# Inverse roots of the row norms on ScalarE, and two moves of turned rows, in a four-layer hybrid kernel

## The reference

```python
def rms_norm(x, g):
    xf = x.astype(jnp.float32)
    y = xf * lax.rsqrt(jnp.mean(xf * xf, axis=-1, keepdims=True) + EPS)
    return (y * g.astype(jnp.float32)).astype(x.dtype)
...
def hybrid_layer(x, c_act, positions, norm_w, w_ada, b_ada, w_in, ret_gn_w, w_proj_attn, w_proj_ret, w_out):
...
    h = rmsnorm(x, norm_w) * (1.0 + scale[:, None, :]) + shift[:, None, :]
    proj = h @ w_in
...
    y_ret = o_ret.astype(x.dtype) * jax.nn.silu(zr)
    merged = jax.nn.sigmoid(ga) * (y_att @ w_proj_attn) + jax.nn.sigmoid(gr) * (y_ret @ w_proj_ret)
    return x + gate[:, None, :] * (merged @ w_out)
```

## Time and profile before

| | us |
|---|---|
| median of three executions | 1066.57 |
| profiled execution, device time | 1068.22 |
| profiled execution, span from first to last instruction | 1066.6 |
| TensorE (PE) busy | 1021.5 |
| VectorE (DVE) busy | 691.5 |
| ScalarE (ACT) busy | 565.2 |
| GpSimd (POOL) busy | 346.8 |

### The profile page before, as it was taken

One profiled execution on the slowest core, in us unless ns is written; L12 is line 12 of the kernel. 1 busy time (PEld: TensorE's weight loads), 2 busy tenths in 40 slices (PEclk: granted clock), 3 DMA queues, 4 the chain that ended last, 5 costly groups with the idle time before them and its releaser, 6 DMA issues.

```text
span 1066.6 us, 15450 instructions
## 1 busy us (share of the span) xinstructions
PE 1021.5 (96%) x6084; PEld 901.6 (85%) x6084; DVE 691.5 (65%) x995; ACT 565.2 (53%) x874; POOL 346.8 (33%) x379
## 2 busy tenths in 40 slices
PE   4899999999999899999999989989999999999996
...
GB/s 269 149 157 90 145 104 111 268 212 233 227 129 180 178 265 225 239 197 158 171 213 180 174 173 202 219 137 199 249 213 217 121 138 178 179 157 140 191 143 40
DMA packets 94441, 191.13 MB, mean 179 GB/s; under 512 B 6769, under 2 KB 10097, under 8 KB 94369
## 3 DMA queue, kind: packets, MB, share of 16 engines
...
HBM read 189.07 MB, written 1.05 MB: 178 GB/s over the span
## 4 chain that ended last, share of the span: by engine, by line
PE 88%; ACT 5%; DVE 4%; POOL 1%; issue 1%; POOLq 0%; DVEq 0%; ACTq 0%
PE G L600 15%; PE G L602 15%; PE G L601 14%; PE G L609 8%; PE G L612 8%; PE G L611 8%; PE B L563 2%; PE G L638 2%; PE G L640 1%; PE G L639 1%; ACT AR L1053 1%; ACT WH L1053 1%; DVE WL L1535 1%; PE B L912 1%; PE B L724 1%
## 5 line engine op out<-in xcount | busy, mean ns | idle before, releaser
L1535 DVE TENSOR_TENSOR WL<-RAW,WH 128x1024 fp32r<-128x1024 f32 (+2 forms) x306 | 397.8, 1304 | 257.1 <-ACT WH L1053 256.4
L1053 ACT ACTIVATE WH<-RAW 128x1024 fp32r<-128x1024 f32 (+2 forms) x306 | 319.9, 1050 | 283.7 <-PE G L602 142.9
L600 PE MATMUL G<-WH,HTh 128*128 128x512 f32 (+1 forms) x564 | 227.9, 404 | 3.0 <-DVE WL L1535 2.8
L609 PE MATMUL G<-HTh,WH 128*128 128x256 f32 x768 | 220.1, 287 | 0.3 <-DVE HTl L1595 0.3
L602 PE MATMUL G<-WL,HTh 128*128 128x512 f32 (+1 forms) x564 | 219.1, 388 | 0.0
L601 PE MATMUL G<-WH,HTl 128*128 128x512 f32 (+1 forms) x564 | 218.5, 387 | 0.0
L611 PE MATMUL G<-HTl,WH 128*128 128x256 f32 x768 | 217.7, 283 | 0.0
L612 PE MATMUL G<-HTh,WL 128*128 128x256 f32 x768 | 217.6, 283 | 0.0
L609 PEld LDWEIGHTS G<-HTh,WH 128*128 128x128 f32 x768 | 146.9, 191 | 2.2 <-issue 2.0
L611 PEld LDWEIGHTS G<-HTl,WH 128*128 128x128 f32 x768 | 147.0, 191 | 0.9 <-issue 0.7
L612 PEld LDWEIGHTS G<-HTh,WL 128*128 128x128 f32 x768 | 146.9, 191 | 0.0
...
## 6 DMA issues: line engine op xcount, KB each, us to landing
...
```

The costliest lines, as they stand in the source:

```text
L600: nc.tensor.matmul(o, xh, wh, start=begins, stop=False)
L609: nc.tensor.matmul(o, fh, h_[:, kx, :], start=begins and f % 2 == 0, stop=False, skip_group_check=True)
L1053: return nc.scalar.activation(out_, ps, ACT.Copy, **kw)
L1535: vt(wl, raw, wh.bitcast(F32), ALU.subtract).then_inc(*dve.mark(LO, n))
```

## The change

**Roots.** GpSimd's `root` is gone. ScalarE has a `root` of two activations on 128x1: the logarithm of (second-half sum + bias), and the exponential of -0.5 times that; the bias is the first-half sum plus 1024 EPS, which VectorE adds in a new `mean` (in layer 0 a constant column). VectorE's Newton step forms its `h` from the same two numbers. An activation table with both functions (`natural_log_exp_and_others`) is loaded at the start of the program and before the squares of each of the four other norms. GpSimd keeps its half of `scaled` in layers 1 to 3. On VectorE the second tile's `rstd` and `scaled` stand before the second `turned` of tile 0, which they followed.

**Layer 0.** VectorE scales all four halves itself. The rows are turned two blocks to a bank, in the order of the pieces that need them: quarters 0 and 1 of both tiles before the first half piece, quarter 2 after half piece 0, quarter 3 after half piece 2. GpSimd clears `H` first and issues its loads after the second half of the input has landed.

**Retention.** `ret_turn` comes after half pieces 177 and 178 instead of 167 and 168, in both hybrid layers.

```diff
 AT_RET = {"scores": (144, 147, 150, 153), "values": (146, 149, 152, 155), "rstd": 158, "gated": (161, 165),
-          "turn": {167: (0, 2), 168: (4, 6)}}
+          "turn": {177: (0, 2), 178: (4, 6)}}
...
+        TURNS = ([(0, ti, r) for r in H4 for ti in L2]
...
-            for q in range(2):
+            def first_turn(r):
                 for ti in range(2):
-                    norm_turn(0, ti, q)
+                    ps = take(("nt", 0, ti, r), HT_LO.of(0, ti, r))
+                    pe.wait_ge(l_ci, 16)
+                    pe.wait_ge(*HN_0.of(ti, r // 2))
+                    for j in range(2):
+                        c = 256 * r + 128 * j
+                        ins = nc.tensor.transpose(ps[:, 128 * j:128 * j + 128], HN[:, ti, c:c + 128], IDENT)
+                    ins.then_inc(*told("nt", 0, ti, r))
+
+            first_turn(0)
+            first_turn(1)
...
                 half(time)
+                if time in (0, 2):
+                    first_turn(2 + time // 2)
...
+            def root(l, ti, last=None):
+
+                act.wait_ge(*(MEAN.of(l, ti) if l else EPS_V.of("e")))
+                if not last:
+                    act.wait_ge(*(SUMSQ.of(l, ti, 1) if l else SUMSQ.of(0, ti)))
+                ss, e = last or NSS[l][:, (2 if l else 0) + ti:(2 if l else 0) + ti + 1], NSE[l][:, ti:ti + 1] if l else eps_col
+                nc.scalar.activation(NLOG[l][:, ti:ti + 1], ss, ACT.Ln, bias=e).then_inc(*act.mark(LOG, l, ti))
+                act.wait_ge(*LOG.of(l, ti))
+                nc.scalar.activation(NR[l][:, ti:ti + 1], NLOG[l][:, ti:ti + 1], ACT.Exp, scale=-0.5).then_inc(
+                    *act.mark(ROOT, l, ti))
+
             def next_layer(l):
 
                 n0 = (0, 54, H0[0], H0[1])[l]
+                nc.scalar.preload_act_table_set("natural_log_exp_and_others")
                 square(l - 1, 0, 0)
                 square(l - 1, 0, 1)
+                root(l, 0)
                 hi(n0 + 1)
                 square(l - 1, 1, 0)
                 hi(n0 + 2)
                 turned(l, 0, 0)
                 square(l - 1, 1, 1)
+                root(l, 1)
...
+            nc.scalar.preload_act_table_set("natural_log_exp_and_others")
             for ti in range(2):
                 act.wait_ge(l_x[ti], 16)
                 nc.scalar.activation(SZA[:, ti, :], X[:, ti, :], ACT.Square,
                                      accum_out=NSS[0][:, ti:ti + 1]).then_inc(*act.mark(SUMSQ, 0, ti))
+                root(0, ti)
+            act.wait_ge(l_cols, 16)
+            turned(0, 0, 0)
             hi(0)
-            act.wait_ge(l_cols, 16)
-            for q in range(2):
+            turned(0, 1, 0)
+            for r in range(1, 4):
                 for ti in range(2):
-                    for r in range(2):
-                        turned(0, ti, 2 * q + r)
-                hi(1 + q)
-            hi(3)
+                    turned(0, ti, r)
+                hi(r)
...
+            nc.scalar.preload_act_table_set("natural_log_exp_and_others")
             square(3, 0, 0)
             square(3, 0, 1)
+            root(4, 0)
             square(3, 1, 0)
...
+            act.wait_ge(*FIN_SQ.of("last"))
+            root(4, 1, ss_last)
...
-            def rstd(l, ti):
+            def mean(l, ti):
+
+                e = NSE[l][:, ti:ti + 1]
+                dve.wait_ge(*SUMSQ.of(l, ti, 0))
+                ts(e, NSS[l][:, ti:ti + 1], 1024 * EPS, None, ALU.add).then_inc(
+                    *(dve.tick() if (l, ti) == (4, 1) else dve.mark(MEAN, l, ti)))
+                if (l, ti) == (4, 1):
+                    dve.wait_ge(*dve.prev)
+                    dve.wait_ge(*SUMSQ.of(4, 1, 1))
+                    ts(e, NSS[4][:, 3:4], e, None, ALU.add).then_inc(*dve.mark(MEAN, 4, 1))
+
+            def rstd(l, ti, last=None):
 
                 k = slice(ti, ti + 1)
                 y = NR[l][:, k]
                 h, z = (x[:, k] for x in (rs_h, rs_z))
-                dve.wait_ge(*MEAN.of(l, ti))
-                ts(h, NSE[l][:, k], -16.0, None, ALU.mult).then_inc(*dve.tick())
+                if l:
+                    dve.wait_ge(*MEAN.of(l, ti))
+                    dve.wait_ge(*(FIN_SQ.of("last") if last else SUMSQ.of(l, ti, 1)))
+                else:
+                    dve.wait_ge(*SUMSQ.of(0, ti))
+                ss, e = last or NSS[l][:, (2 if l else 0) + ti:(2 if l else 0) + ti + 1], NSE[l][:, k] if l else eps_col
+                ts(h, ss, e, -16.0, ALU.add, ALU.mult).then_inc(*dve.tick())
                 dve.wait_ge(*dve.prev)
                 dve.wait_ge(*ROOT.of(l, ti))
                 stt(z, y, h, y, ALU.mult, ALU.mult).then_inc(*dve.tick())
...
                 residual(l - 1, 0, 1)
+                mean(l, 0)
                 residual(l - 1, 1, 0)
                 rstd(l, 0)
                 scaled(l, 0)
                 residual(l - 1, 1, 1)
+                mean(l, 1)
                 lo(n0 + 1)
                 turned(l, 0, 0)
+                rstd(l, 1)
+                scaled(l, 1)
                 turned(l, 0, 1)
                 lo(n0 + 2)
-                rstd(l, 1)
-                scaled(l, 1)
                 lo(n0 + 3)
                 turned(l, 0, 2)
...
+            nc.vector.memset(eps_col, 1024 * EPS).then_inc(*dve.mark(EPS_V, "e"))
             nc.vector.memset(M3[:, :, :, :].rearrange("p a b c -> p (a b c)"), 0.0).then_inc(*dve.mark(S5_V, "zero"))
+            dve.wait_ge(*EPS_V.of("e"))
             for ti in range(2):
                 rstd(0, ti)
-                scaled(0, ti)
+                dve.wait_ge(*RSTD.of(0, ti))
+                for q in range(2):
+                    c = slice(512 * q, 512 * q + 512)
+                    ts(HN[:, ti, c], X[:, ti, c], NR[0][:, ti:ti + 1], None, ALU.mult).then_inc(*dve.mark(HN_0, ti, q))
+            turned(0, 0, 0)
             lo(0)
-            for q in range(2):
+            turned(0, 1, 0)
+            for r in range(1, 4):
                 for ti in range(2):
-                    for r in range(2):
-                        turned(0, ti, 2 * q + r)
-                lo(1 + q)
-            lo(3)
+                    turned(0, ti, r)
+                lo(r)
...
+            mean(4, 0)
...
+                    mean(4, 1)
+                    rstd(4, 1, ss_last)
...
-            def root(l, ti):
-
...
-                gtt(y, e, neg_half, ALU.pow).then_inc(*pool.mark(ROOT, l, ti))
...
+            for r in range(2):
+                nc.gpsimd.memset(H[r].rearrange("p a b -> p (a b)"), 0.0).then_inc(*pool.tick())
+            pool.wait_ge(l_x[1], 16)
             nc.gpsimd.dma_start(BR, t["s5_b"]).then_inc(l_br, 16)
             nc.gpsimd.dma_start(CR, t["s5_c"]).then_inc(l_cr, 16)
-            nc.gpsimd.dma_start(CS[:, 0, :].bitcast(I32), t["pos"].partition_broadcast(P)).then_inc(l_pos, 16)
             nc.gpsimd.dma_start(TRI, const("tri")).then_inc(l_tri, 16)
             nc.gpsimd.dma_start(SBM, const("sbmask")).then_inc(l_sbm, 16)
-            for r in range(2):
-                nc.gpsimd.memset(H[r].rearrange("p a b -> p (a b)"), 0.0).then_inc(*pool.tick())
```

55 lines of the change are left out of this document (17 added, 38 removed).

## The result

The changed kernel takes **1059.3 us** (median of four runs, 1058.2 to 1059.4), the kernel before 1066.6 (median of three, 1065.6 to 1068.2). A fourth execution of the kernel before, of 2611.84 us, is left out of every figure here. The ratio of the means is 0.9928, with a 95% interval of 0.9908 to 0.9947: 7.7 us less (7.3 by the medians). The forecast was 1055.0, with a range of 1050.5 to 1059.5. The direction was right and the time lies 0.2 us inside the range, but the size was not right: 4.3 us of the gain are missing.

The account below looks back on a forecast made before the run. PE was taken as the bound, busy 1021.5 of 1066.6 us, so only its waits and slow clock count. Terms summed to -11.8 from 1068.2, giving 1056.4, lowered to 1055.0 for slow stretches; range 1050.5 to 1059.5.

Parts of the forecast that it names:

- The step that failed: Opening: VectorE scales four halves at 0.49 us each, so tile 1 is scaled at about 10 us.
- The term: Opening, layer 0: 1.0 us gained in all, with bounds of 6 gained and 3 lost.
- That last sign: Near 50 us: PE waits 6 us or more before the weight piece that waited 2.85, losing its earlier lead.
- The next step: Opening: first half piece at 12 us gains 1 us by ScalarE's chain; at 15.5 it loses 2 to 3.
- Retention, -7.2: Layer 2 retention turn: 3.9 us of PE's wait for the gate go, and 3.4 us of slow clock.
- the new wait for weights: Layer 2 retention, half piece 168: a stretched weight split makes PE wait 1.0 us anew.
- the slower rival: Half piece 184 waits for turned retention in both hybrid layers, 4.9 + 3.4 us each: 1070.5; chance 0.03.
- the rival in which the stall re-forms: Layer 2 retention: a weight wait before half pieces 168 and 172, with slow clock; price 3.5, 1058.5 us; chance 0.12.
- Turns and end, -3.6: Turns to layer 1 +0.4, layer 2 -0.7, layer 3 -2.0, and the end after the last matmul -1.3 us.
- Layer 2: Turn to layer 2: second turned block 0.6 us later, tile 1's scaled rows 2 us earlier; -0.7 us net.
- The rival in which roots in ScalarE's queue cost PE at each turn: Turns between layers: second roots delay turned rows by 0.6 us each; 5.6 us more, 1060.6; chance 0.07.
- opening counts in full: Opening: ScalarE catches up from 24 to 49 us, so 5 us more are gained: 1050; chance 0.08.

Follow-up runs that it names:

- clears_early: The changed kernel with GpSimd's four clears moved ahead of its wait for the second input tile; 1055.7 us, ratio 0.9886.
- retention_only: The kernel before with only the retention turn moved to half pieces 177 and 178; 1060.5 us, ratio 0.9934.
- retention_back: The changed kernel with the retention turn put back to half pieces 167 and 168; 1065.9 us, ratio 0.9985.
- order_alone: The changed kernel with layer 1's second root, and VectorE's refinement and scaling of tile 1, behind the second turned block; 1058.6 us, ratio 0.9919.
- all_pairs_first: clears_early with all four pairs of turned blocks ahead of the first half piece; 1054.7 us, ratio 0.9883.
- loads_on_path: The changed kernel without table loads ahead of the squares, so the compiler places them at the roots; 1081.1 us, ratio 1.0131.

## Why the prediction was right in direction and too large

**The step that failed** is in the opening: "VectorE's scaling is 0.49 us for each half, four of them instead of two. With them tile 1 is scaled at about 10." The row is true, but in it GpSimd was not clearing. The change moved GpSimd's clears behind its loads, right beside tile 1's scaling; those two took 4.23 us, and tile 1 was scaled at 13.05. clears_early, which takes only this away, has the forecast's first half piece and exponential, and against the old opening nearly its gain (-0.8 for -1.0). The term came out at +2.8, 3.8 above the forecast, and three of the forecast's own signs show it: the first half piece at 15.37 and not at 12 to 13, the exponential at 27.04 and not at 22 to 25, the weight wait 3.74 and not 6 or more.

That last sign was wrong by itself. "What PE gains before 49 it waits out there" does not hold even in clears_early: PE is 6.0 us ahead at its first half piece and 1.5 ahead at 45 us, and waits 3.72. The lead went in late turned blocks, in half pieces at 1.2 GHz and in small waits for weights. It cost nothing, since the wait's end was set by ScalarE all the same.

The next step did hold: the text gave 1 gained "from 12" and "from 15.5 it makes 2 to 3 lost". The first half piece came at 15.37 and 2.8 were lost. But 15.5 was tied to the landing of the weights, as a bound, and not to VectorE, so the likelier way to it was left out.

I had the rule at hand and applied it in one place only. The trace shows that a VectorE scaling of one SBUF tile was held until the last of four clears ended. The Trainium skill ("SBUF — State Buffer", "Who interferes with whom") says that `tensor_scalar` can run in a mode that uses both port pairs, and that whichever of it and a GpSimd instruction starts first makes the other block fully. The trace agrees on the block. It does not agree on who wins, as far as its starts tell: the second scaling started at 9.78, before the first clear at 9.96, and still ended after all four. In the earlier trace rows it could not be seen, since VectorE's scaling stood behind GpSimd's root, and the root behind the clears.

**Retention, -7.2**: the mechanism was right, and the size came out (-7.0 in the traces, -6.1 to -7.0 by retention_only, -6.6 by retention_back), but by luck: two errors of the sum cancel. The slow clock was priced at 3.4 us over the whole 7.00 us of the earlier trace rows, though PE is busy only 4.69 of them and stands in its wait for the rest, where a slow clock costs nothing; 4.69 x 0.5 gives 2.3. And the new wait for weights, 1.0 in the forecast, is 1.26 where it appears, but the changed kernel's trace has none. So that trace has 4.9 + 2.1 = 7.0, and retention_only's, with the wait, 5.8. No wait appeared behind half piece 184, so the slower rival fell, and the rival in which the stall re-forms too.

**Turns and end, -3.6**: -4.0 by the medians; -4.6 by the traces without layer 3's retention, and -3.0 of that without the slow stretch that only the profiled execution of the kernel before had. Layer 3 (-2.0) came out as worked. At the end the sum did (-1.3), its parts did not: 1.2 ahead of the last squares where 0.7 was told, 0.2 behind them where 0.6 was. Layer 2 was to give -0.7 and gave -2.1: PE's waits there hardly changed (1.53, 0.96 and 0.54 us, against 1.45, 0.47 and 1.31), but from 361 to 365 us the granted clock is 1.00 where it was 0.57 before, which is 4.00 x 0.43 = 1.7 us. That is not the change's: retention_only has the old turn and 1.00 as well, and -1.6 against the same trace. Against retention_only the turn gives -0.6, so the -0.7 was right. Layer 1 was to give +0.4 and gave +0.8; order_alone, where the first wait shrinks by 0.62 with the second root's place, bears out the cause of the longer wait. A root on ScalarE takes 0.62 us with the hand-over, 0.5 in the forecast. The rival in which roots in ScalarE's queue cost PE at each turn fell.

**The rival "opening counts in full"** fell, and all_pairs_first shows why even a good opening can't count in full: ScalarE is full up to 60 us.

**The account of the 4.3 us.** 3.8 are the opening and 0.4 is layer 1; each of the other terms came within 0.3, once the slow stretch at 361 us is set apart. That stretch is what I had guessed at: I took 1.4 us more off the sum because the profiled execution of the kernel before lay 1.6 above the median and slow stretches might come and go. It cost that execution 1.6 us, it is in none of the traces above or below but that of loads_on_path, where more was slow, and the changed kernel's profiled execution lies within 0.1 of its median. So this step was right, though a guess.

**A version that beats both.** With the clears ahead, all turns ahead of the half pieces and the second root of layer 1 behind the turned block, the kernel takes 1051.7 us (layer1_order; 0.9859 of the kernel before, 0.9844 to 0.9874), 7.6 us less than the changed kernel. The same with blocks of four takes 1052.2, and blocks of four without the root's move 1052.6, so the gain is that of the clears and of the turns.
